# Opening stage: conditioning by feature tile on four column tiles of TensorE, with four projection units run tile by tile

## The chip, the cores and the metric

The kernel runs on one core of one Trainium2 chip. The metric is the device time of one execution in microseconds (us), the median of several runs. The core has five engines that run their own instruction streams and wait for each other by semaphores: TensorE (PE in the profile, its weight loads PEld), VectorE (DVE), ScalarE (ACT), GpSimd (POOL) and SyncE (SP, which issues nearly all transfers here).

## The reference, cut to what matters

Two transformer-like layers over 256 tokens of 1024 features. The change touches the start of the first:

```python
c_act = jax.nn.silu(c)                        # c: (1, 1024)
mod = c_act @ ada_w + ada_b                   # ada_w: (1024, 6144)
sh1, sc1, gt1, sh2, sc2, gt2 = jnp.split(mod, 6, axis=-1)
h = rmsnorm(x, mix_pre_g) * (1.0 + sc1) + sh1 # x: (256, 1024)
proj = h @ w_in                               # w_in: (1024, 10272)
```

Of `mod`, `h` needs the first two of six parts, 2048 columns of `ada_w` (8 MiB in fp32). Everything else in the layer needs `h`.

## The kernel before, in words

Activations lie feature-major: a tile is 128 features on the partitions by 256 tokens. The 1024 features of `x` and `h` are eight such tiles. The output features of each projection are cut into blocks of 128; one **unit** is such a block, computed from one chunk of weights of 128 x 1024 fp32 (512 KiB). Chunks pass through a ring of four slots: SP loads one (`load`), ACT rounds it to the matmul format (`high`, L1042, into `WH`), POOL subtracts to get the rest (`low`, L503, into `WL`), and PE multiplies. `h` is split the same way into `HH` and `HL`. A `triple` is the three matmuls `WH*HH`, `WH*HL`, `WL*HH` of one feature tile; a unit is eight triples, 24 matmuls, into one of four PSUM banks `psL`. SP loads a slot again once its chunk is split; ACT splits into a slot again once the unit that used it is done and its bank is read.

The opening, before: SP puts all transfers into one queue in the order of L407 to L430. ACT takes the silu of `c`, broadcast to all partitions, into `psO` (L1082). DVE takes each of 16 tiles of transposed `ada_w` (128 output features by 1024) as it lands, multiplies it with that row and sums (L1634); the sixteen sums are `mod[:, 0:16]`. From the tenth product's count on, PE runs 20 matmuls on constants whose result nobody reads (`fill`, L681). PE also sums the squares of `x` (`stat`, L678), ACT makes the reciprocal root of it (L1086, L1087). Once all sixteen products are there, DVE adds the bias, makes the gain `lead`, and `h` is made tile by tile by DVE, ACT and DVE (L1644, L1074, L1649). PE runs units 0 and 1 together, tile by tile as `h` is made (`together`, L603), then units 2 to 23 one after the other. Unit 24 follows behind a small projection `dt` (24 matmuls into `psS`). The first stage of the layer's projection, with its convolution on ACT (L1099) and DVE (L1676), runs beside these units, and with it DVE multiplies further tiles of `ada_w` with the row in `psO` (L1628).

## Time and profile before

| | |
|---|---|
| median of 3 runs | 1103.64 us (1101.42, 1103.64, 1114.60) |
| the profiled execution | 1113.12 us |
| its span, first to last instruction | 1111.3 us |
| mean granted clock of TensorE in it | 0.986 of full speed |
| PE busy | 1051.7 us, 95% of the span |
| DVE, ACT, POOL busy | 51%, 58%, 62% |
| DMA: bytes, mean rate over the span | 226.84 MB, 204 GB/s |

The profiled execution lies 9.5 us above the median of the runs and within their spread. All durations below are from it. Busy time of PE counts overlapping matmuls as busy once; it says when PE had work, not how well it used it.

### The profile page before, as it was taken

The numbers are of one execution on the slowest core, as the hardware profiler recorded it, in microseconds if no ns is written. First come the engines' busy times: TensorE is split into PE (matmuls) and PEld (weight loads), VectorE is DVE, ScalarE is ACT, GpSimd is POOL, SyncE is SP. The second block draws the span as 40 slices with busy tenths as digits, with TensorE's granted clock in tenths as the row PEclk, the third lists the DMA queues.
The fourth block names the chain that finished last, engine by engine and source line by source line (L and its number), as shares of the span: only waits on it lengthen the run. The fifth ranks groups of instructions, "written<-read, shape, count | busy, mean of one in ns | idle before, by whom it ended". The sixth has DMA issues, their size and how long they took to land.

```text
span 1111.3 us, 22886 instructions
## 1 busy us (share of the span) xinstructions
PE 1051.7 (95%) x8357; PEld 993.7 (89%) x8357; DVE 562.8 (51%) x1165; ACT 642.6 (58%) x1140; POOL 692.6 (62%) x306
## 2 busy tenths in 40 slices
PE   3999999999899989999999999998998889999998
PEld 2999999988789979999998999896665689999998
DVE  5877425589774454555423432495263724444400
ACT  3555754477764576666546557735576546666532
POOL 0787888812268847888786487660220065888795
PEclk9999999999999999999999999999899999999999
DMA  9988677656427855676677387567211033555463
GB/s 372 380 283 287 245 292 285 224 184 209 168 99 268 263 204 171 228 242 223 217 258 252 110 286 278 174 206 293 98 40 38 1 117 129 195 186 188 162 208 106
DMA packets 63650, 226.84 MB, mean 204 GB/s; under 512 B 6976, under 2 KB 8160, under 8 KB 63328
## 3 DMA queue, kind: packets, MB, share of 16 engines
q1 hardware_dynamic: 62384, 221.74, 57.1%
q10 hardware_dynamic: 1200, 4.23, 1.3%
q8 instruction: 40, 0.66, 0.2%
q14 instruction: 26, 0.21, 0.1%
HBM read 224.86 MB, written 1.08 MB: 203 GB/s over the span
## 4 chain that ended last, share of the span: by engine, by line
PE 67%; issue 16%; POOL 8%; ACT 3%; DMA 2%; DVE 2%; SPq 1%; POOLq 0%; ACTq 0%; DVEq 0%
PE psL L550 64%; POOL WL L503 8%; DMA R<-ada_w 1%; PE psS L550 1%; PE psO L550 1%; DMA ring<-wts 1%; SPq L405 1%; ACT WH L1042 1%; ACT R L1153 0%; ACT L1033 0%; ACT HR L1074 0%; SPq L390 0%; POOL R L530 0%; PE psS L839 0%; DVE HR L1649 0%
## 5 line engine op out<-in xcount | busy, mean ns | idle before, releaser
L503 POOL TENSOR_TENSOR WL<-ring,WH 128x1024 fp32r<-128x1024 f32 (+1 forms) x282 | 672.2, 2398 | 306.4 <-ACT WH L1042 245.5
L550 PE MATMUL psL<-HR,WH 128*128 128x256 f32 x3056 | 545.4, 281 | 5.7 <-POOL WL L503 2.5
L550 PEld LDWEIGHTS psL<-HR,WH 128*128 128x128 f32 x3056 | 468.2, 188 | 10.3 <-POOL WL L503 4.4
L550 PE MATMUL psL<-HR,WL 128*128 128x256 f32 x1528 | 428.1, 280 | 0.0
L550 PEld LDWEIGHTS psL<-HR,WL 128*128 128x128 f32 x1528 | 288.3, 189 | 0.0
L1042 ACT ACTIVATE WH<-ring 128x1024 fp32r<-128x1024 f32 (+1 forms) x210 | 216.1, 1040 | 100.9 <-PE psL L550 84.5
L550 PE MATMUL psL<-RR,WH 128*128 128x256 f32 x1344 | 240.8, 282 | 6.1 <-POOL WL L503 4.5
L550 PEld LDWEIGHTS psL<-RR,WH 128*128 128x128 f32 x1344 | 206.9, 189 | 7.7 <-issue 3.9
L550 PE MATMUL psL<-RR,WL 128*128 128x256 f32 x672 | 188.8, 281 | 0.0
L1328 ACT ACTIVATE WH<-ring 128x1024 fp32r<-128x1024 f32 (+1 forms) x88 | 92.9, 1055 | 86.8 <-PE psL L550 86.8
L1909 DVE SCALAR_TENSOR_TENSOR CT<-psL,par,CT 128x254 f32<-128x254 f32 (+1 forms) x176 | 81.0, 480 | 116.7 <-ACT CT L1331 111.3
L1628 DVE SCALAR_TENSOR_TENSOR adaring<-adaring,psO 128x1024 f32<-128x1024 f32 x80 | 96.8, 1217 | 70.9 <-DMA adaring<-ada_w 66.8
L550 PEld LDWEIGHTS psL<-RR,WL 128*128 128x128 f32 x672 | 127.1, 189 | 0.0
L550 PE MATMUL psL<-WH,HR 128*128 128x256 f32 (+1 forms) x320 | 55.0, 279 | 0.7 <-DVE HR L1649 0.7
L530 POOL TENSOR_TENSOR R<-R 128x256 f32<-128x256 f32 x16 | 14.5, 907 | 57.8 <-DVE R L1758 57.8
L550 PEld LDWEIGHTS psL<-WH,HR 128*128 128x128 f32 x320 | 48.6, 188 | 1.0 <-issue 0.9
L1331 ACT ACTIVATE CT<-psL,par 128x256 f32<-128x256 f32 x88 | 48.2, 548 | 0.0
L550 PE MATMUL psS<-SQ,par 128*128 128x256 f32 x90 | 27.9, 471 | 20.5 <-ACT SQ L1084 14.9
L550 PE MATMUL psL<-WL,HR 128*128 128x256 f32 (+1 forms) x160 | 44.5, 278 | 0.0
L550 PEld LDWEIGHTS psS<-SQ,par 128*128 128x128 f32 x90 | 20.7, 239 | 25.9 <-issue 17.5
L2222 DVE SCALAR_TENSOR_TENSOR X<-psL,mod,X 128x256 f32<-128x256 f32 x16 | 7.7, 484 | 67.9 <-PE psL L550 67.6
L1676 DVE SCALAR_TENSOR_TENSOR R<-psL,par,R 128x255 f32 (+2 forms) x72 | 34.7, 481 | 14.3 <-DVE R L1676 13.5
(255 smaller groups left out, 1103.5 us busy)
## 6 DMA issues: line engine op xcount, KB each, us to landing
ring<-wts SPq DMA_DIRECT2D x289, 512.0 KB, 3.7
adaring<-ada_w SPq DMA_DIRECT2D x80, 512.0 KB, 4.8
R<-ada_w SPq DMA_DIRECT2D x16, 512.0 KB, 12.6
ring<-wts SPq DMA_DIRECT2D x16, 384.0 KB, 3.4
R<-cum_dram ACTq DMA_DIRECT2D x8, 512.0 KB, 4.3
ring<-wts SPq DMA_DIRECT2D x8, 288.0 KB, 3.7
adaring<-wts SPq DMA_DIRECT2D x1, 2048.0 KB, 9.4
WHF<-wts SPq DMA_DIRECT2D x2, 1024.0 KB, 7.8
```

The source lines that it names most:

```text
L405: sp.dma_start(ADA0[n], ada_w[n * P:(n + 1) * P, :]).then_inc(ada_first[n], 16)
L503: nc.gpsimd.tensor_tensor(WL[:, k, 0:n], ring[:, k, 0:n], WH[:, k, 0:n].bitcast(F32), SUB).then_inc(lo_done, 1)
L530: G.tensor_tensor(Z[:, j, :], XBC[:, j, :], Z[:, j, :], MUL).then_inc(y_ready, 1)
L550: return nc.tensor.matmul(out, lhsT, rhs, start=start, stop=stop)
L1042: A(WH[:, k, 0:n], ring[:, k, 0:n], ACT.Copy).then_inc(hi_done, 1)
L1328: A(WH[:, q % SLOTS, 0:n], ring[:, q % SLOTS, 0:n], ACT.Copy).then_inc(hi_done, 1)
L1331: A(CT[:, 2 * slot + b, :], psL[:, u % 4, 0:T], ACT.Identity, scale=par[:, bass.ds(w0 + 2 * 44 + b * KF + j + it, 1)], bias=par[:, bass.ds ...
L1628: V.scalar_tensor_tensor(w, w, 1.0, cond, MUL, MUL, accum_out=col).then_inc(ada_used, 1)
L1676: ins = V.scalar_tensor_tensor(dst, psL[:, (u0 + k) % 4, 0:T - back], par[:, bass.ds(m + (c_w + (3 - back) * NXBC), 1)], dst, MUL, ADD)
L1909: ins = V.scalar_tensor_tensor(dst, psL[:, us[b] % 4, 0:T - back], par[:, bass.ds(w0 + (2 - back) * 44 + b * KF + j + it, 1)], dst, MUL, ADD)
L2222: V.scalar_tensor_tensor(X[:, m, :], lin(u), gates[:, m:m + 1], X[:, m, :], MUL, ADD).then_inc(lin_free[u % 4], 1)
```

## The change

The sixteen tiles of `ada_w` become eight of 1 MiB. Each holds, for one feature tile of `h`, its 128 columns of shift and 128 of gain, with the 1024 inputs in eight groups on the partitions. `CPAD` holds the silu of `c` as eight columns, each padded with zeros to 32. `ada_row(j)` multiplies them on PE: 32 x 256 outputs, the eight groups on four column tiles of the array in turn, so that four partial sums lie at partitions 0, 32, 64 and 96 of a bank of `psS`. ACT copies them to SBUF (`ROW`); `ada_col(j)` turns and sums them with two matmuls against a column of ones; DVE adds the bias and makes the gain of that tile, and tile `j` of `h` is made at once. `first_units(k)` runs the triples of feature tile `k` for units 0 to 3 together. The row of silu values that stays in `psO` for the later products is now made from eight diagonal blocks (DVE) and two matmuls with ones (`cond_rows`), no longer by a transfer of `c` to all partitions. Chunks 1 and 3 are subtracted by DVE (`first_low`) instead of POOL. The `fill` matmuls go. The transfers are reordered, and the parameters come in three parts instead of two.

```diff
--- before.py
+++ after.py
@@ -146,10 +146,11 @@
 
 PAR_SPEC = [
 
-    ("c_2", 8), ("ada_b", 48), ("mix_pre_g", 8), ("ones", P),
-
-    ("ident", P), ("w_dt", KD * HEADS1), ("mix_post_g", 8),
-    ("xconv_w", 4 * NXBC), ("xconv_b", NXBC), ("dskip", 16), ("ssd_norm_g", 16), ("sconv_w", 24),
+    ("c_1", 8), ("c_2", 8), ("ada_b", 48), ("mix_pre_g", 8), ("ones", P), ("ident", P),
+
+    ("xconv_w", 4 * NXBC), ("xconv_b", NXBC), ("w_dt", KD * HEADS1),
+
+    ("mix_post_g", 8), ("dskip", 16), ("ssd_norm_g", 16), ("sconv_w", 24),
...
-PAR_FIRST = PAR["ident"][0]
-
-
-def build(nc, x_t, par_in, c_row, ada_w, wts, out_t):
+PAR_FIRST, PAR_MID = PAR["xconv_w"][0], PAR["mix_post_g"][0]
+
+
+def build(nc, x_t, par_in, ada_w, wts, out_t):
...
-        ADA0 = [R[:, n * ADA_COLS + (0 if n < 14 else 4096):(n + 1) * ADA_COLS + (0 if n < 14 else 4096)] for n in range(ADA_FIRST)]
-        CROW = R[:, 20480:21504]
+        ADA0 = [R[:, n * 2048 + (0 if n < 7 else 4096):(n + 1) * 2048 + (0 if n < 7 else 4096)] for n in range(KD)]
+        DIAG1 = CT[:, :, :].rearrange("p a b -> p (a b)")
+        CPAD = RS[:, 1, :].rearrange("p (k m) -> p k m", m=32)
+        ROW = region(SQ, 0, a=2, b=T)
...
                     else:
-                        sp.wait_ge(lo_done, PLAN.split_at[before] + 1 + i * per)
+                        sp.wait_ge(lo_done, max(PLAN.split_at[before] + 1, SLOTS) + i * per)
...
-
-            sp.dma_start(CROW, c_row.rearrange("a b -> (a b)").partition_broadcast(P)).then_inc(c_in, 16)
+                rows = ada_w[n * 2 * P:(n + 1) * 2 * P, :].rearrange("(p a) n -> p (a n)", a=2)
+                sp.dma_start(ADA0[n], rows).then_inc(ada_first[n], 16)
+
             sp.dma_start(par[:, 0:PAR_FIRST], par_in[:, 0:PAR_FIRST]).then_inc(par_in_sem, 16)
-            for n in range(4):
-                load_first(n)
             sp.dma_start(X[:, :, :], x_t).then_inc(x_in, 16)
-            for n in range(4, 10):
-                load_first(n)
             load(0)
-            for n in range(10, 13):
-                load_first(n)
+            load_first(0)
             load(1)
-            for n in range(13, 16):
-                load_first(n)
+            sp.dma_start(par[:, PAR_FIRST:PAR_MID], par_in[:, PAR_FIRST:PAR_MID]).then_inc(par_mid_in, 16)
+            load_first(1)
             load(2)
             load(3)
-            sp.dma_start(par[:, PAR_FIRST:NPAR], par_in[:, PAR_FIRST:NPAR]).then_inc(par2_in, 16)
+            for n in range(2, KD):
+                load_first(n)
             load(4)
             load(5)
+            sp.dma_start(par[:, PAR_MID:NPAR], par_in[:, PAR_MID:NPAR]).then_inc(par2_in, 16)
             load_ada(16)
...
-            lows(0, PAIR_Q)
+            low(0)
+            low(2)
+            lows(SLOTS, PAIR_Q)
...
-            def cond_rows(diag):
-
-                pe.wait_ge(diag_ready, 1)
+            def cond_rows(diag, use):
+
+                pe.wait_ge(diag_ready, use)
                 for half in range(2):
...
+            cond_rows(DIAG1, 1)
             pe.wait_ge(sq_ready, 1)
             stat("stat_mix", sq_at, 8)
-            for n in range(12, 17):
-                pe.wait_ge(ada_used, n)
-                fill(0, 4)
-            linear8("in1", 0, 24, h_hi, h_lo, from_count(h_ready, 0), 2)
+
+            def ada_row(j):
+
+                pe.wait_ge(cpad_ready, 1)
+                pe.wait_ge(ada_first[j], 16)
+                if j >= 1:
+                    pe.wait_ge(col_read, j)
+                for k in range(KD):
+                    r = 32 * (k % 4)
+                    last = mm(psS[r:r + 32, 1, 0:T], CPAD[:, k, :], ADA0[j][:, k * T:(k + 1) * T], k < 4, k >= 4)
+                last.then_inc(row_done, 1)
+
+            def ada_col(j):
+
+                pe.wait_ge(row_ready, j + 1)
+                for e in range(2):
+                    last = mm(psS[:, 1, T + e:T + e + 1], ROW[:, j % 2, e * P:(e + 1) * P], pv("ones", 0, 1), True, True)
+                last.then_inc(col_done, 1)
+
+            def first_units(k):
+
+                pe.wait_ge(h_ready, k + 1)
+                if k == 0:
+                    pe.wait_ge(lo_done, SLOTS)
+                for c in range(SLOTS):
+                    last = triple(psL[:, c, 0:T], WH[:, c, k * P:(k + 1) * P], WL[:, c, k * P:(k + 1) * P],
+                                  HH[:, k, :], HL[:, k, :], k == 0, k == 7)
+                    if k == 7:
+                        last.then_inc(lin_done, 1)
+
+            for j in range(KD):
+                ada_row(j)
+                if 2 <= j < 7:
+                    first_units(j - 2)
+                if j == 7:
+                    first_units(6)
+                ada_col(j)
+                if j == 6:
+                    first_units(5)
+            first_units(7)
+            linear8("in1", SLOTS, 24 - SLOTS, h_hi, h_lo)
...
-            act.wait_ge(consts_ready, 1)
+            act.wait_ge(consts_ready, 2)
+            A(CPAD[:, :, 0:1].rearrange("p k m -> p (k m)"), pv("c_1"), ACT.Silu).then_inc(cpad_ready, 1)
             A(csil[:, :], pv("c_2"), ACT.Silu).then_inc(csil_ready, 1)
-            act.wait_ge(c_in, 16)
-            A(psO[:, :, :].rearrange("p a b -> p (a b)"), CROW, ACT.Silu).then_inc(cbc_ready, 1)
             act.wait_ge(x_in, 16)
             A(SQ[:, :], wide(X[:, :, :]), ACT.Square).then_inc(sq_ready, 1)
+            high(0)
             act.wait_ge(s_done, SCRATCH["stat_mix"] + 1)
             st.link(A(RS[:, 0, :], sbank("stat_mix")[:, 0:T], ACT.Ln, scale=1.0 / D, bias=eps_col[:, :]))
             A(sbank("stat_mix")[:, 0:T], RS[:, 0, :], ACT.Exp, scale=-0.5).then_inc(rs_ready, 1)
-            for c in range(2):
-                high(c)
-            make_hh(mod[:, 0:8], 0, first_t)
+
+            for j in range(KD):
+                act.wait_ge(row_done, j + 1)
+                A(ROW[:, j % 2, :], psS[:, 1, 0:T], ACT.Copy).then_inc(row_ready, 1)
+                act.wait_ge(t_ready, j + 1)
+                A(HH[:, j, :], CT[:, j % 4, :], ACT.Identity, bias=mod[:, j:j + 1]).then_inc(hh_ready, 1)
+                if j == 0:
+                    high(1)
+                if j == 1:
+                    high(2)
+                    high(3)
+                if j == 3:
+                    act.wait_ge(par_mid_in, 16)
+                    A(WDT[:, 0, :], pv("w_dt"), ACT.Copy).then_inc(wdt_hi, 1)
             fed[0] = SLOTS
-            act.wait_ge(par2_in, 16)
-            A(WDT[:, 0, :], pv("w_dt"), ACT.Copy).then_inc(wdt_hi, 1)
...
+            def diagonals(diag, silu):
+
                 for k in range(KD):
-                    st.mark(V.tensor_scalar(diag[:, k * P:(k + 1) * P], pv("ident"), csil[:, k:k + 1], None, MUL))
+                    st.mark(V.tensor_scalar(diag[:, k * P:(k + 1) * P], pv("ident"), silu(k), None, MUL))
...
-            dve.wait_ge(cbc_ready, 1)
-            for n in range(ADA_FIRST):
-                first = n + 8 if n < 8 else n - 8
-                dve.wait_ge(ada_first[n], 16)
-                V.scalar_tensor_tensor(ADA0[n], ADA0[n], 1.0, cond, MUL, MUL, accum_out=mod[:, first:first + 1]
-                                       ).then_inc(ada_used, 1)
-
-            def make_h(shift, gains, rs, base, t_at=None):
-
-                slots = 2 if t_at else 4
+            def make_h(shift, gains, rs, base):
+
                 for j in range(KD + 1):
                     if j < KD:
-                        if j >= slots:
-                            dve.wait_ge(h_ready, base + j - slots + 1)
-                        V.scalar_tensor_tensor(t_at(j) if t_at else CT[:, j % 4, :], X[:, j, :], gains[:, j:j + 1], rs, MUL,
+                        if j >= 4:
+                            dve.wait_ge(h_ready, base + j - 3)
+                        V.scalar_tensor_tensor(CT[:, j % 4, :], X[:, j, :], gains[:, j:j + 1], rs, MUL,
                                                MUL).then_inc(t_ready, 1)
                     if j >= 1:
                         n = j - 1
                         dve.wait_ge(hh_ready, base + n + 1)
-                        V.scalar_tensor_tensor(HL[:, n, :], t_at(n) if t_at else CT[:, n % 4, :], shift[:, n:n + 1], HH[:, n, :].bitcast(F32),
+                        V.scalar_tensor_tensor(HL[:, n, :], CT[:, n % 4, :], shift[:, n:n + 1], HH[:, n, :].bitcast(F32),
                                                ADD, SUB).then_inc(h_ready, 1)
 
-            dve.wait_ge(ada_used, ADA_FIRST)
             dve.wait_ge(par_in_sem, 16)
-            V.tensor_tensor(mod[:, 0:16], mod[:, 0:16], pv("ada_b", 0, 16), ADD).then_inc(mod_ready, 1)
-            dve.wait_ge(mod_ready, 1)
-            st.link(V.scalar_tensor_tensor(lead[:, 0:8], mod[:, 8:16], 1.0, pv("mix_pre_g"), ADD, MUL))
-            dve.wait_ge(x_in, 16)
-            dve.wait_ge(rs_ready, 1)
-            make_h(mod[:, 0:8], lead[:, 0:8], sbank("stat_mix")[:, 0:T], 0, first_t)
+            dve.wait_ge(cpad_ready, 1)
+            diagonals(DIAG1, lambda k: CPAD[:, k, 0:1])
+
+            def first_low(c):
+
+                dve.wait_ge(hi_done, c + 1)
+                V.tensor_tensor(WL[:, c, :], ring[:, c, :], WH[:, c, :].bitcast(F32), SUB).then_inc(lo_done, 1)
+
+            rows2 = lambda view, j: view.rearrange("p (a b) -> p a b", b=KD)[:, :, j:j + 1].rearrange("p a b -> p (a b)")
+            for j in range(KD):
+                dve.wait_ge(col_done, j + 1)
+                V.tensor_tensor(rows2(mod[:, 0:16], j), psS[:, 1, T:T + 2], rows2(pv("ada_b", 0, 16), j), ADD).then_inc(col_read, 1)
+                dve.wait_ge(col_read, j + 1)
+                st.link(V.scalar_tensor_tensor(lead[:, j:j + 1], mod[:, 8 + j:9 + j], 1.0, pv("mix_pre_g", j, 1), ADD, MUL))
+                if j == 0:
+                    dve.wait_ge(cbc_ready, 1)
+                    dve.wait_ge(x_in, 16)
+                    dve.wait_ge(rs_ready, 1)
+                V.scalar_tensor_tensor(CT[:, j % 4, :], X[:, j, :], lead[:, j:j + 1], sbank("stat_mix")[:, 0:T], MUL,
+                                       MUL).then_inc(t_ready, 1)
+                dve.wait_ge(hh_ready, j + 1)
+                V.scalar_tensor_tensor(HL[:, j, :], CT[:, j % 4, :], mod[:, j:j + 1], HH[:, j, :].bitcast(F32),
+                                       ADD, SUB).then_inc(h_ready, 1)
+                if j < 2:
+                    first_low(2 * j + 1)
+                if j == 4:
+                    dve.wait_ge(par_mid_in, 16)
+                    dve.wait_ge(wdt_hi, 1)
+                    V.tensor_tensor(WDT[:, 1, :], pv("w_dt"), WDT[:, 0, :].bitcast(F32), SUB).then_inc(wdt_ready, 1)
             dve.wait_ge(t_ready, 8)
             dve.sem_inc(s_free[SCRATCH["stat_mix"] % 2], 1)
-            dve.wait_ge(par2_in, 16)
-            dve.wait_ge(wdt_hi, 1)
-            V.tensor_tensor(WDT[:, 1, :], pv("w_dt"), WDT[:, 0, :].bitcast(F32), SUB).then_inc(wdt_ready, 1)
-            V.tensor_copy(identb[:, :], pv("ident")).then_inc(consts_ready, 1)
-            V.tensor_copy(maskb[:, :], pv("causal_add")).then_inc(consts_ready, 1)
+            dve.sem_inc(mod_ready, 1)
+            dve.sem_inc(ada_used, ADA_FIRST)
...
-    return np.concatenate([a[D:2 * D], a[0:D], a[2 * D:], b])
+    w = i["ada_w"][0][:, 0:2 * D].reshape(KD, P, 2, KD, P)
+    return np.concatenate([w.transpose(3, 1, 0, 2, 4).reshape(2 * D, D), a[2 * D:], b])
```

Not shown: new semaphores and their counts, `diagonals` called for the second layer as before, two small casts and the wait for the last part of the parameters moved behind the first loop of convolutions.

PE's first rows, before (`psS<-SQ,par` is `stat`, `psL<-par` is `fill`, `psL<-HR,WH` and `psL<-HR,WL` are the triples of `together`):

```order
L547 UNCONDITIONAL_BRANCH
L550 MATMUL psS<-SQ,par 128x256 x8
L550 MATMUL psL<-par 128x128 x20
L550 MATMUL psL<-HR,WH 128x256 x2
L550 MATMUL psL<-HR,WL 128x256
```

And with the change (`psO<-CT,par` is `cond_rows`, `psS<-R,RS` is `ada_row`, `psS<-par,SQ` is `ada_col`):

```order
L550 MATMUL psO<-CT,par 128x512 x2
L550 MATMUL psS<-SQ,par 128x256 x8
L550 MATMUL psS<-R,RS 32x256 x8
L550 MATMUL psS<-par,SQ 128x1 x2
L550 MATMUL psS<-R,RS 32x256 x8
L550 MATMUL psS<-par,SQ 128x1 x2
L550 MATMUL psS<-R,RS 32x256 x8
L550 MATMUL psL<-HR,WH 128x256 x2
L550 MATMUL psL<-HR,WL 128x256
```

`ada_row` of tiles 0, 1 and 2 stands ahead of the first triple; `ada_col` of tile 2 stands behind the four triples of feature tile 0.

ACT's rows from the silu on, before (`SQ<-X` the squares, `RS` and `psS<-RS` the root, `WH<-ring` is `high`, `HR<-psL,mod` makes `HH`):

```order
L1080 ACTIVATE csil<-par 128x8
L1082 ACTIVATE psO<-R 128x1024
L1084 ACTIVATE SQ<-X 128x2048
L1086 ACT_TABLE_LOAD
L1086 ACTIVATE RS<-psS,eps_col 128x256
L1087 ACT_TABLE_LOAD
L1087 ACTIVATE psS<-RS 128x256
L1042 ACTIVATE WH<-ring 128x1024 x2
L1074 ACTIVATE HR<-psL,mod 128x256 x3
```

And with the change, from the squares on (`SQ<-psS` is the copy into `ROW`):

```order
L1119 ACTIVATE SQ<-X 128x2048
L1080 ACTIVATE WH<-ring 128x1024
L1122 ACT_TABLE_LOAD
L1122 ACTIVATE RS<-psS,eps_col 128x256
L1123 ACT_TABLE_LOAD
L1123 ACTIVATE psS<-RS 128x256
L1127 ACTIVATE SQ<-psS 128x256
L1129 ACTIVATE HR<-CT,mod 128x256
L1080 ACTIVATE WH<-ring 128x1024
L1127 ACTIVATE SQ<-psS 128x256
L1129 ACTIVATE HR<-CT,mod 128x256
L1080 ACTIVATE WH<-ring 128x1024 x2
```

Chunk 0 is rounded ahead of the root, chunk 1 behind tile 0 of `h`, chunks 2 and 3 behind tile 1; the copy of a tile's sums stands behind the previous tile's `HH`.

## Rows read from the trace of the kernel before

**Rows 1.** Busy time by stage; columns: busy us of each engine, PEclk, DMA share, GB/s.
```profile
20.00:40.00 20.00, 14.90 (x83) 12.82 (x83) 16.52 (x34) 9.85 (x16) 8.19 (x4) 0.83 1.02 414
```

**Rows 2.** Chain of waits in the opening: start us, us, what; matmuls counted.
```profile
15.44 15.33 DMA R<-ada_w
...
39.77 63.87 PE psL L550 x540
103.63 2.77 PE psS L550 x24
```

**Rows 3.** SP's first issues of ada_w (start, us), and issues with us to landing.
```profile
1.66 1.90 SPq L405 DMA_DIRECT2D R<-ada_w  x4
...
R<-ada_w SPq DMA_DIRECT2D x1, 512.0 KB, 4.8
...
par<-params SPq DMA_DIRECT2D x1, 96.0 KB, 4.0
```

**Rows 4.** Timeline of ACT and PE (start us, us); last, durations of four `stat` records.
```profile
12.87 1.91 ACT L1084 ACTIVATE SQ<-X 128x2048 f32<-128x2048 f32 x1 [6.49 <-DMA X<-x_t]
...
14.92 6.64 PE L550 MATMUL psS<-SQ,par 128*128 128x256 f32 x16 [14.92 <-ACT SQ L1084]
...
21.60 0.47 ACT L1086 ACTIVATE RS<-psS,eps_col 128x256 f32<-128x256 f32 x1 [5.52 <-PE psS L550]
...
23.39 0.39 ACT L1087 ACTIVATE psS<-RS 128x256 f32<-128x256 f32 x1
...
L550 PE MATMUL psS<-SQ,par x4: 379/458/635, 20.2 to 21.2; 128*128 128x256 f32 x4
```

**Rows 5.** Groups by line and shape: busy us, mean ns of one, idle before.
```profile
L1617 DVE TENSOR_SCALAR HX<-par,csil 128x128 f32<-128x128 f32 x8 | 1.6, 271 | 0.0
...
L1654 DVE TENSOR_TENSOR mod<-mod,par 128x16 f32<-128x16 f32 x1 | 0.2, 175 | 0.0
...
L1644 DVE SCALAR_TENSOR_TENSOR psL<-X,lead,psS 128x256 f32<-128x256 f32 x8 | 3.8, 489 | 0.2
...
L1649 DVE SCALAR_TENSOR_TENSOR HR<-psL,mod,HR 128x256 fp32r<-128x256 f32 x8 | 3.8, 481 | 0.2
...
L1074 ACT ACTIVATE HR<-psL,mod 128x256 fp32r<-128x256 f32 x8 | 3.7, 471 | 6.3 <-DVE psL L1644 6.3
...
L1343 ACT ACTIVATE RR<-psS 128x256 f32 x32 | 11.9, 372 | 0.0
...
L1099 ACT ACTIVATE R<-psL,par 128x256 f32 x24 | 13.5, 563 | 29.0 <-PE psL L550 29.0
...
L1042 ACT ACTIVATE WH<-ring 128x1024 fp32r<-128x1024 f32 x195 | 203.8, 1055 | 79.6 <-PE psL L550 63.3 <-issue 9.3 <-DMA ring<-wts 2.9
```

**Rows 6.** Subtractions of 128 x 1024 on DVE (ns min/median/max), and one on POOL.
```profile
L1764 DVE TENSOR_TENSOR WL<-ring,WH x16: 1212/1224/1226, 234.0 to 290.2; 128x1024 fp32r<-128x1024 f32 x16
...
L1816 DVE TENSOR_TENSOR RR<-R,RR x4: 1211/2836/3194, 307.9 to 328.3; 128x1024 fp32r<-128x1024 f32 x4
...
38.91 2.39 POOL L503 TENSOR_TENSOR WL<-ring,WH 128x1024 fp32r<-128x1024 f32 x1 [0.47 <-ACT WH L1042]
```

**Rows 7.** Fp32 matmuls with 32 columns of weights (ns min/median/max), then a timeline.
```profile
L550 PE MATMUL psL<-adaring,HX x32: 378/379/404, 779.9 to 781.4; 128*32 128x256 f32 x32
L550 PE MATMUL psL<-WHF,HX x32: 378/379/380, 781.6 to 783.2; 128*32 128x256 f32 x32
...
786.08 0.63 PE L550 MATMUL psS<-par,SQ 128*128 128x30 f32 x4 [0.82 <-ACTq L1483]
786.64 0.64 PE L550 MATMUL psL<-ring,HX 128*32 128x256 f32 x8
```

**Rows 8.** Short stretches around changes of the granted clock; columns as in rows 1.
```profile
24.20:24.40 0.20, 0.00 (x0) 0.00 (x0) 0.15 (x3) 0.20 (x1) 0.00 (x0) 0.79 0.92 369
31.00:31.20 0.20, 0.20 (x3) 0.20 (x3) 0.20 (x1) 0.00 (x0) 0.00 (x0) 0.65 1.02 410
...
796.00:804.00 8.00, 8.00 (x37) 7.57 (x37) 3.04 (x9) 2.12 (x9) 0.00 (x0) 0.50 0.00 1
```

34 lines of the change are left out of this document (17 added, 17 removed).

## The prediction

> **What bounds the kernel now.** I read three views in this order. The busy times by stage show where PE is not full: over the span it is busy 95%, and between 20 and 40 us only 14.9 of 20 us [rows 1], with the transfers at their limit. The chain of waits shows why: up to 30.8 us it hangs on the last tile of `ada_w`, and from 39.77 us it is one unbroken run of 540 matmuls on PE, then `dt` [rows 2]. That run gives the unit's price, 24 x 63.87 / 540 = 2.84 us, and an anchor: `dt` begins at 103.6 us, 20 units behind the start of unit 4, so **unit 4 starts at 103.6 - 20 x 2.84 = 46.9 us**. From there PE is the chain, and the change leaves the units from 4 on as they are. So its whole effect is the shift of unit 4's start.
>
> **Transfers.** The first tile of `ada_w` lands at 1.66 + 4.8 = 6.5 us, the sixteenth at 30.8 [rows 2, 3]; between them 9.5 MiB go through the queue (7.5 of `ada_w`, 1 of `x`, two chunks), 2.56 us per MiB. `x` lands at 12.9 [rows 4]. The change puts 11.34 MiB up to its last tile instead of 10.59 (`c` broadcast away, two chunks and 0.25 of parameters more), so tile 7 lands at 30.8 + 0.75 x 2.56 = 32.7 us. Backwards by the same rate: tile 6 at 30.1, tile 2 at 19.9, tile 1 at 14.8, tile 0 at 10.5, chunks 2 and 3 by 17.3, `x` at 6.6. The first parameters, which took 4.0 us behind another transfer [rows 3], I put at 4.1.
>
> **Removed.** The sixteen products on DVE wait for transfers and hide behind them; without them nothing starts earlier, since their place is taken by the steps below. The `fill` matmuls fill idle time; what they cover is the clock, below. Each is priced at nothing by itself.
>
> **Up to the first tile of h.** Silu and hops 0.3, eight diagonals 1.6 [rows 5]: `cond_rows` starts at about 6.1. It streams half the columns that `stat` streams, and `stat` took 6.64 us at the lower clock level (1.2 GHz: its records last 635 ns, against 379 at the end, at 2.4) [rows 4], so 3.3 us, to 9.4. Squares are ready at 6.6 + 1.9 = 8.5, so `stat` waits for `cond_rows`. In the run before, the short records come some 6 us after PE began. From 6.1 that is 12, so `stat` takes 2.6 us slow and 2.0 fast: 14.0. From its end to the root are 23.39 + 0.39 - 21.6 = 2.2 us [rows 4]: 16.2. `ada_row(0)` is done under it; the copy (0.37) [rows 5] brings 16.6, `ada_col` (nearest row: four narrow fp32 records in 0.63 [rows 7]) 17.3. Then bias, gain, `t`, `HH`, `HL` at 0.17, 0.17, 0.49, 0.47, 0.48 [rows 5] with 0.2 of hops, 2.0 us: tile 0 of `h` at 19.3.
>
> **The new wait.** Triples may start only when four low parts are done. ACT does chunk 1 behind `HH(0)`: 18.8 to 19.9 [rows 5]. Then its copy for tile 1, `ada_col(1)` to 20.9; DVE is meanwhile in `first_low(1)`, 1.22 us [rows 6], to 21.1; `HH(1)` ends at 22.5, chunks 2 and 3 are rounded by 23.6 and 24.7. POOL's low part of chunk 2 takes 2.4 us, to 26.0 [rows 6]. DVE's of chunk 3 overlaps it. A DVE subtraction of that size with both inputs in SBUF takes 1.22 us while POOL does nothing, and 2.8 in the middle where POOL subtracts too [rows 6]; so I let it start when POOL ends: **first triples at 27.2 us**. Queued behind that wait on PE stand `ada_col(2)` and all later tiles, although tile 6 has nearly landed. PE had `ada_row(2)` at 21.3 and then nothing for almost 5 us. Before, the clock fell at 24.3, 2.7 us after `stat` [rows 4, 8]; so it is at the lower level here.
>
> **The loop from then on.** Per tile, PE does `ada_row`, 12 matmuls, `ada_col`, and waits for DVE's bias step before the next `ada_row`. Column tiling is in the trace: 32 records with 32 columns of weights start every 1.7 us [rows 7], so 16 take 0.87 us, a quarter of full width. Twelve matmuls are 1.42 us; with 0.63 and 0.2 for `ada_col` and the bias, the period is **3.1 us at full clock, above the 2.56 of a transfer**: this loop is bound by PE's own round trip, and ACT (0.9 us per tile) and DVE (2.0) fit in it. At the lower level the 12 matmuls take 2.84; of `ada_row` no row shows its price there, between 0.87 (if the weight loads set it) and 1.75; I take 1.75, since full-width matmuls at that level take twice as long, and that is the nearer operation than a weight load. So: triples 0 to 30.0, bias of tile 2 at 30.9, `ada_row(3)` to 32.6. There the clock rises, some 5.5 to 6 us after the work began, as before [rows 4, 8]. Triples 1 and the column give 34.8; tiles 4 and 5 at 3.1 each, 41.0. Then `ada_row(6)` 41.9, triples 4 43.3, triples 5 behind the column 45.1, `ada_row(7)` and triples 6 47.4, column 48.0, tile 7 of `h` 50.0, unit 0 done 50.5.
>
> **Behind the loop.** All four banks and slots come free together. Unit 4 needs bank 0 read (0.56), chunk 4 rounded (1.05) and subtracted (2.4), 4.1 with hops [rows 5, 6], three of them with PE idle: **unit 4 at 54.6 us**. Before, this handover was hidden, because units 0 and 1 ended before 2 and 3. Chunk 4 lands at 34.0 and waits; the following chunks, at 2.4 per low part against 2.84 per unit, keep up.
>
> **Sum.** 54.6 - 46.9 = **+7.7 us**. Against the profiled execution that is 1120.8; it lies 9.5 above the median, so the forecast is 1103.6 + 7.7 = **1111 us**.
>
> **A rule against the trace.** In the trace, 32-column matmuls start at 786.64 while full-width ones run until 786.71 [rows 7]: I see no pause at the switch, and charge none. The Trainium skill (TensorEngine Tiling (Array Packing), Key Properties) says that changing the tiling mode drains TensorE. By that rule each of the two switches per tile would cost the tail of a record, 0.38 less the 0.21 between two starts at full clock (half of 6.64 / 16 [rows 4, 7]), 0.17 us, and the five periods on the path would make the sum 9.4 instead of 7.7; this is an estimate with that page's rule and the 379 ns of the row.
>
> **Rivals.**
> - *The clock does not fall, or DVE and POOL do not collide.* Triples at 26.0 and full clock bring `ada_row(3)` to 28.2, three periods bring `ada_row(6)` to 37.5 instead of 41.0, then the same tail: unit 4 at 51.1, **+4.2, 1108**. With only one of the two it is +5.4 to +6.5. For it: PE has small pieces of work between 17 and 22. Against: 5 us without any.
> - *The transfers set the pace after all* (faster). If the low parts are done by 20 us and a period fits into 2.56, the triples ride on the landings: tile 7 at 32.7, row and triples 6 to 35.0, column 35.6, `h` 37.6, unit 0 done 38.1, handover 4.1: unit 4 at 42.2, **-4.7, 1099**. It needs the period below 2.56, a step cheaper than every row says, and the chain to the fourth low part 6 us shorter. It decides at the first triple: below 20 us with the short period it is a gain; with a period of 3.1 the start would have to be before 22.
> - *The clock stays at 1.2 GHz through the loop* (slower). Between 796 and 804 us the engine works without a pause and stays at 0.50 [rows 8], in small matmuls as `ada_col` and `ada_row` are. Period 1.75 + 2.84 + 0.8 = 5.4: `ada_row(3)` at 30.9, `ada_row(6)` at 47.1, tile 7 of `h` at 62.1, unit 0 done 63.0, unit 4 at 67.1: **+20.2, 1124**. If it lasts one more unit, 2.84 us more, it passes 2%. Against: the idle-time matmuls raised it at 31.1 [rows 8], and this loop keeps PE as busy as they did.
>
> **How the numbers follow.** Forecast 0.47, first rival (all its variants) 0.25, faster rival 0.13, slow clock 0.11 (a third of it in its long form), something else 0.04. The range runs from 1099 to 1120: it takes in the forecast with either price of the unknowns, the first rival, and the runs' own spread (1101 to 1115 for one kernel), and about half of the faster rival; it leaves the slow clock out. A difference counts as measured here beyond 2%, 22 us. No case reaches -22, and only the long form of the slow clock +22: faster 0.01, within 0.95, slower 0.04.
>
> **What would show it.** In the new profile: the first triple at 26 to 27.5 us and the fourth low part just before it; the idle of PE ahead of it; the granted clock at 0.5 there; `ada_row` starts 3.1 us apart, not 2.56; PE idle for about 3 us before unit 4; `dt` at 111, not 103.6. A first triple near 20 us, or periods of the landings' length, would refute the forecast.

## The result: 3% slower

The changed kernel takes **1137.23 us** (median of 4 runs, 1135.99 to 1138.22); the kernel before took 1109.12 beside it (4 runs, 1101.42 to 1114.74). The ratio is **1.0313**, 95% interval 1.0248 to 1.0378. Forecast were 1111 us and a range to 1120, with 0.04 for this side. The prediction was wrong.

The chain of waits of the changed kernel from the handover on; its second and third rows answer to the last two of [rows 2] (start us, us, what; matmuls counted). Behind it stands the row of the kernel before that answers to its fourth:

```profile
54.69 2.35 POOL WL L501
...
57.09 59.34 PE psL L550 x480
116.43 2.74 PE psS L550 x24
119.18 115.20 PE psL L550 x960
```

```profile
106.41 113.08 PE psL L550 x960
```

Unit 4 starts at 57.09 us; before it was 46.9, so the opening is 10.2 us longer up to there (forecast 7.7). `dt` begins at 116.43 instead of 103.63: 12.8 later. But the span is 24.3 us longer (1135.6 against 1111.3), so about half the loss is *behind* the opening, in code that the change leaves alone: the 960 matmuls behind `dt` alone take 115.20 us instead of 113.08. Four stretches of steady matmuls show it. The kernel before, and then the changed one (us from:to, length, busy time and records of PE, then of the weight loads, DVE, ACT, POOL; granted clock, DMA share, GB/s):

```profile
65.00:95.00 30.00, 30.00 (x258) 30.00 (x257) 21.87 (x44) 15.99 (x21) 25.49 (x12) 1.00 0.86 286
120.00:160.00 40.00, 40.00 (x342) 40.00 (x341) 13.85 (x21) 28.55 (x39) 34.65 (x15) 1.00 0.77 280
500.00:600.00 100.00, 100.00 (x851) 100.00 (x850) 38.56 (x80) 57.02 (x88) 83.91 (x38) 1.00 0.70 239
1010.00:1090.00 80.00, 80.00 (x681) 80.00 (x681) 22.51 (x52) 41.42 (x61) 67.38 (x31) 1.00 0.55 182
```

```profile
65.00:95.00 30.00, 30.00 (x252) 30.00 (x251) 21.90 (x46) 16.33 (x22) 25.45 (x11) 1.00 0.85 280
120.00:160.00 40.00, 40.00 (x336) 40.00 (x335) 19.76 (x33) 29.61 (x43) 30.29 (x14) 1.00 0.69 245
500.00:600.00 100.00, 100.00 (x835) 100.00 (x834) 44.27 (x94) 57.38 (x93) 81.88 (x37) 1.00 0.67 228
1010.00:1090.00 80.00, 80.00 (x669) 80.00 (x668) 30.70 (x72) 46.16 (x75) 66.06 (x29) 1.00 0.54 178
```

PE has no idle time and the clock is at 1.00 in all eight rows, and yet 1.8 to 2.3% fewer matmuls fit into each: three of them take 0.360 us from start to start instead of 0.353. No busy share says this; only the count beside it does.

The opening itself, on PE (start, us, operation, records; last, idle time before it and what ended it). The eight fp32 matmuls of an `ada_row` leave sixteen records:

```profile
8.79 4.50 PE L550 MATMUL psS<-SQ,par 128*128 128x256 f32 x16
13.22 1.07 PE L550 MATMUL psS<-R,RS 128*32 128x256 f32 x16
...
20.54 1.94 PE L550 MATMUL psS<-R,RS 128*32 128x256 f32 x16 [0.35 <-DVE mod L1703]
26.24 0.77 PE L550 MATMUL psL<-HR,WH 128*128 128x256 f32 x2 [3.76 <-DVE WL L1698]
28.94 0.85 PE L550 MATMUL psS<-par,SQ 128*128 128x1 f32 x4
30.13 1.94 PE L550 MATMUL psS<-R,RS 128*32 128x256 f32 x16 [0.34 <-DVE mod L1703]
...
35.46 1.07 PE L550 MATMUL psS<-R,RS 128*32 128x256 f32 x16 [0.35 <-DVE mod L1703]
36.46 0.50 PE L550 MATMUL psL<-HR,WH 128*128 128x256 f32 x2
...
38.00 0.50 PE L550 MATMUL psS<-par,SQ 128*128 128x1 f32 x4
38.85 1.07 PE L550 MATMUL psS<-R,RS 128*32 128x256 f32 x16 [0.35 <-DVE mod L1703]
...
51.81 0.79 PE L550 MATMUL psL<-HR,WH 128*128 128x256 f32 x2 [2.03 <-DVE HR L1713]
57.09 0.50 PE L550 MATMUL psL<-HR,WH 128*128 128x256 f32 x2 [2.35 <-POOL WL L501]
```

The first triples wait 3.76 us for a low part and start at 26.24. The rows of 32-column matmuls take 1.94 us at the lower clock and 1.07 at the full one; at full clock the next one starts 3.39 us later. DVE's low parts, whose second one runs beside POOL's from 22.67 to 25.01:

```profile
18.89 1.23 DVE L1698 TENSOR_TENSOR WL<-ring,WH 128x1024 fp32r<-128x1024 f32 x1 [0.46 <-ACT WH L1080]
...
23.57 2.52 DVE L1698 TENSOR_TENSOR WL<-ring,WH 128x1024 fp32r<-128x1024 f32 x1 [1.41 <-ACT WH L1080]
```

1.23 us alone, 2.52 beside POOL, of which 1.44 lie under POOL's: what is left after POOL's end is 1.08. The Trainium skill (SBUF — State Buffer, "SBUF: two separate sides") says that such a subtraction and a GpSimd operation take the ports that they share by turns and whole. These rows agree but for 0.15 us: by that rule a whole subtraction, 1.23, would be left, and 1.08 is. The granted clock (columns as above):

```profile
20.00:34.00 14.00, 9.54 (x58) 6.97 (x59) 5.21 (x10) 3.56 (x6) 2.34 (x1) 0.50 1.02 420
34.00:36.00 2.00, 1.65 (x21) 1.48 (x23) 0.78 (x3) 0.00 (x0) 0.00 (x0) 0.88 1.02 426
36.00:50.00 14.00, 13.09 (x136) 10.70 (x128) 4.87 (x16) 3.76 (x9) 0.00 (x0) 1.00 0.65 259
...
52.00:54.00 2.00, 2.00 (x10) 2.00 (x11) 0.04 (x1) 0.90 (x2) 0.00 (x0) 0.50 0.00 0
...
58.00:60.00 2.00, 2.00 (x13) 2.00 (x12) 1.64 (x4) 0.81 (x1) 2.00 (x2) 0.59 0.82 260
60.00:62.00 2.00, 2.00 (x12) 2.00 (x11) 1.20 (x4) 0.16 (x1) 2.00 (x2) 0.56 0.72 225
```

It is at the lower level (1.2 GHz) from about 18 to 34 us, and falls twice more: in the last triples, behind the 2 us that PE waited for `h`, and in unit 4, behind the waits of the handover.

### The profile page after: what moved, and what is told of

The parts are those of the page before. It is cut to its first block, busy times and chain, and to the rows that moved or that the text cites. A ratio compares the mean times of both kernels' runs of the same rounds, so it can differ in the third digit from the quotient of the medians.

```text
span 1135.6 us, 23102 instructions
## 1 busy us (share of the span) xinstructions
PE 1079.9 (95%) x8481; PEld 1015.2 (89%) x8481; DVE 550.5 (48%) x1158; ACT 644.3 (57%) x1148; POOL 685.4 (60%) x304
## 3 DMA queue, kind: packets, MB, share of 16 engines
HBM read 224.34 MB, written 1.08 MB: 199 GB/s over the span
## 4 chain that ended last, share of the span: by engine, by line
PE 66%; issue 20%; POOL 8%; ACT 3%; DVE 1%; DMA 1%; POOLq 0%; ACTq 0%; DVEq 0%; SPq 0%
PE psL L550 63%; POOL WL L501 8%; PE psS L550 1%; PE psO L550 1%; DMA ring<-wts 1%; ACT WH L1080 0%; DMA X<-x_t 0%; ACT R L1199 0%; ACT L1071 0%; POOL R L530 0%; PE psS L877 0%; DVE CT L1943 0%; DVE X L1944 0%; ACT RS L1069 0%; ACT RS L1071 0%
## 5 line engine op out<-in xcount | busy, mean ns | idle before, releaser
L501 POOL TENSOR_TENSOR WL<-ring,WH 128x1024 fp32r<-128x1024 f32 (+2 forms) x280 | 665.0, 2389 | 337.1 <-ACT WH L1080 270.1
L550 PE MATMUL psL<-HR,WH 128*128 128x256 f32 x3056 | 560.5, 284 | 12.4 <-POOL WL L501 4.6
L550 PEld LDWEIGHTS psL<-HR,WH 128*128 128x128 f32 x3056 | 477.9, 191 | 19.5 <-issue 8.7
L550 PE MATMUL psL<-HR,WL 128*128 128x256 f32 x1528 | 434.9, 285 | 0.0
L550 PE MATMUL psL<-RR,WH 128*128 128x256 f32 x1344 | 243.8, 283 | 5.4 <-POOL WL L501 4.1
L1929 DVE TENSOR_TENSOR CT<-CT,psS 128x256 f32<-128x256 f32 x21 | 8.8, 421 | 65.0 <-ACT psS L1331 59.5
L550 PE MATMUL psL<-ring,R 128*128 128x192 f32 (+1 forms) x128 | 31.5, 395 | 2.2 <-DMA ring<-wts 2.2
```

Source lines behind the costliest of these rows:

```text
L501: nc.gpsimd.tensor_tensor(WL[:, k, 0:n], ring[:, k, 0:n], WH[:, k, 0:n].bitcast(F32), SUB).then_inc(lo_done, 1)
L550: return nc.tensor.matmul(out, lhsT, rhs, start=start, stop=stop)
L1929: ins = V.tensor_tensor(SUMS, SUMS, psS[:, m % 2, 0:T], ADD).then_inc(sq_added, 1)
```

## The experiments

Sixteen kernels ran, in four groups; each group was timed beside its own runs of the kernel before, each group on another chip, and only ratios to those are compared. What could make an untouched stream of matmuls slower? The change also makes `par` 8 columns wider (c_1 is added), so every buffer behind it in SBUF (X, SQ, the buffer HR of HH and HL, R, CT, RS) moves by 32 bytes, while the weight buffers ring, WH, WL and `adaring` stay ahead of it. **Theory L**: this shift costs the stream. **Rival O**: the opening costs everything.

**First group: dead columns, and two units.**

`e1`, the kernel before (`e2` has 16 in place of 8):

```diff
-        par = sb("par", [P, NPAR])
+        par = sb("par", [P, NPAR + 8])
```

> The kernel before, with the parameter buffer 8 columns (32 bytes per partition) longer, nothing read there. In the changed kernel the parameters grew by 8 columns, and everything behind them in SBUF (x, h, the large work buffer) lies 32 bytes further on. Layout theory: this alone makes every matmul that streams from those buffers slower, as in the changed kernel (836 matmuls in 100 us instead of 851), so this kernel is slower than before by 12 to 16 us, 1.012 to 1.014. Rival, the change's own instructions cause the slower pace: no difference, 1.000.

Measured: **1.0219** (1.0149 to 1.0289). Eight columns that nothing reads cost the kernel before 2.2%, more than the 1.2 to 1.4% expected. Its stretches are those of the changed kernel:

```profile
65.00:95.00 30.00, 30.00 (x252) 30.00 (x251) 21.40 (x44) 16.01 (x22) 25.27 (x11) 1.00 0.81 277
...
500.00:600.00 100.00, 100.00 (x836) 100.00 (x835) 41.72 (x88) 55.99 (x88) 81.81 (x37) 1.00 0.68 230
```

> The kernel before with the parameter buffer 16 columns (64 bytes) longer: the control of the 32-byte shift. Layout theory, if it is the 64-byte phase that counts: 1.000, and 851 matmuls in 100 us as before. If any shift costs: slower as with 8 columns.

Measured: 1.0119 (1.0042 to 1.0195), with 252 and 845 records in these stretches. A place at a multiple of 64 bytes is not what it needs.

`e3`, the changed kernel with the same edit, so that it too lies 64 bytes off:

> The changed kernel with the parameter buffer 8 columns longer, which puts the buffers behind it back on the 64-byte phase they had before. Layout theory: 12 to 16 us faster than the changed kernel, so 9 to 12 us slower than before, 1.009 to 1.011, the opening's own loss (unit 4 starts at 57.1 instead of 46.9). Rival: as the changed kernel, 1.022 to 1.031.

Measured: 1.0202 (1.0136 to 1.0269). Divided by 1.0119, that of `e2` with the same shift, the change proper is 1.008.

`e4`, as `e3`, but only units 0 and 1 in the loop, and all low parts on POOL:

```diff
-                    pe.wait_ge(lo_done, SLOTS)
-                for c in range(SLOTS):
+                    pe.wait_ge(lo_done, 2)
+                for c in range(2):
...
             first_units(7)
+            for c in (2, 3):
+                unit(c, c, 1, h_hi, h_lo)
...
-            low(0)
-            low(2)
-            lows(SLOTS, PAIR_Q)
+            lows(0, PAIR_Q)
...
-                if j < 2:
-                    first_low(2 * j + 1)
```

> The changed kernel, buffers back on the old phase, but only units 0 and 1 run tile by tile in the loop; units 2 and 3 follow as in the kernel before, and all four low parts are POOL's. The first triple waits for two low parts instead of four (about 21 us instead of 26.2), a period of the loop has 6 matmuls less per tile (2.7 instead of 3.4 us), and the rounding of chunk 4 is hidden behind units 2 and 3. Theory that the loop's four units cost the opening its gain: unit 4 starts at 43 to 45 us, 2 to 4 us earlier than before, 0.996 to 0.998. Rival, the conditioning on PE itself (waits between PE, ACT and DVE, the low clock) is too slow: unit 4 at 47 or later, 1.000 or more.

Measured: 1.0176 (1.0095 to 1.0256). The first triples start at 21.70, as expected, but from tile 1 on an `ada_row` takes 1.94 us, the tiles come 4.5 to 5.3 us apart, and `dt` begins at 115.72: 0.7 us earlier than with the change, 1.4 earlier than in `e3`, and 12 later than before. So the rival's side holds. The clock stays at 0.50 from 20 to 34 and at 0.55 from 34 to 48, although PE is busy 92 to 94% of that time:

```profile
20.00:34.00 14.00, 12.85 (x78) 8.54 (x73) 6.17 (x11) 4.65 (x9) 5.20 (x3) 0.50 1.02 427
34.00:48.00 14.00, 13.16 (x85) 9.06 (x85) 4.31 (x14) 2.68 (x6) 0.00 (x0) 0.55 0.76 309
```

**Second group: where the address counts.**

`e5`, the changed kernel with `par` at 3785 columns again, so that all large buffers lie where they lay before; c_2 is loaded straight into `csil`, and its silu comes behind `dt`:

```diff
-    ("c_1", 8), ("c_2", 8), ("ada_b", 48), ("mix_pre_g", 8), ("ones", P), ("ident", P),
+    ("c_1", 8), ("ada_b", 48), ("mix_pre_g", 8), ("ones", P), ("ident", P),
...
-    ("cmask_add", 2 * NCMP), ("cmask01", 2 * NCMP), ("sel", 2 * NCMP),
+    ("cmask_add", 2 * NCMP), ("cmask01", 2 * NCMP), ("sel", 2 * NCMP), ("c_2", 8),
...
-        par = sb("par", [P, NPAR])
+        par = sb("par", [P, NPAR - 8])
...
+            sp.dma_start(csil[:, :], par_in[:, NPAR - 8:NPAR]).then_inc(par2_in, 16)
...
-            A(csil[:, :], pv("c_2"), ACT.Silu).then_inc(csil_ready, 1)
+            A(csil[:, :], csil[:, :], ACT.Silu).then_inc(csil_ready, 1)
```

> The changed kernel with every large SBUF buffer at the address it has in the kernel before: of the 16 columns that carry the two conditioning vectors, c_2's 8 are kept in the small buffer csil and loaded on their own, so that par is 3785 columns wide again. Theory L (the addresses cost the rest): the matmul stream goes back to 851 records in 500:600, the start of 'dt' stays about 116, and the median is 10 to 13 us above the kernel before (ratio 1.009 to 1.012). Rival O (the opening costs all of it and what follows is only a side of it): the median stays 25 to 28 us above (ratio 1.023 or more), at about 836 records in 500:600.

Measured: **1.0092** (1.0057 to 1.0128). Theory L's number; O falls. And 1.0092 x 1.0219 (`e1`) = 1.0313, the ratio of the change; that all the digits agree is luck, since the factors are uncertain by 0.4 and 0.7%. The chain from unit 4 on:

```profile
54.68 56.31 PE psL L551 x480
110.99 2.72 PE psS L551 x24
```

Unit 4 starts at 54.68, 2.4 us earlier than with the change. The first triples started 1.4 us earlier (24.82) and the last ones 2.0 (49.78), and the last ones ran at full clock; from the end of unit 0 on the handover takes 4.0 us in both. Two things came out against the forecast: `dt` at 111 instead of about 116, and a stream that is quicker than before, 267 records in 65:95 against 258 and 871 in 500:600 against 851. The profiled execution is also the quickest of this kernel's eleven (1107.28, median 1123.29); its pace is taken up with the table below.

`e6`, 8 dead columns ahead of all buffers; `e7`, 8 behind HR's buffer; `e8`, `par` 32 wider, all in the kernel before:

```diff
+        lead_pad = sb("lead_pad", [P, 8])
         ring = sb("ring", [P, SLOTS, SLOT])
```

> The kernel before with a dead buffer of 8 columns (32 bytes) ahead of all SBUF buffers, so that the weights WH and WL and the activations HH and HL move together and keep their distances. If the distance between the weights and the activations is what the matmul stream feels, the time is that of the kernel before (within 0.3%) and 851 records in 500:600. If it is the place of a buffer by itself (a multiple of 64 bytes, say), it is slower by 1 to 2%, as with 32 bytes behind par (1.022).

```diff
         HX = sb("HX", [P, 4096])
+        pad_r = sb("pad_r", [P, 8])
```

> The kernel before with 8 dead columns (32 bytes) behind the buffer of HH and HL: par, X, SQ, HH and HL stay, the buffer R of the activations (Z, XBC, G1, XTOK), CT and RS move by 32 bytes. If the addresses of HH and HL are what costs, no change in 500:600 if that stretch multiplies HH and HL. If it is the results in R, CT and RS, the whole loss of 1 to 2% is here.

```diff
-        par = sb("par", [P, NPAR])
+        par = sb("par", [P, NPAR + 32])
```

> The kernel before with par 32 columns (128 bytes) wider: everything behind par keeps its place within 128 bytes. If the pattern repeats by 128 bytes, the time is that of the kernel before; if not, it is 1 to 2% slower as with 32 (1.022) and 64 bytes (1.012).

Measured: `e6` 0.9963 (0.9926 to 0.9999), `e7` 1.0009 (0.9971 to 1.0047), `e8` **0.9837** (0.9793 to 0.9880). Moving everything together costs nothing, so it is not a buffer's place by itself but a distance. Moving R, CT and RS costs too little to see in the whole time, but the trace of `e7` shows it. Its first row below multiplies HH and HL, which did not move, its second a tile of R, which did; the rows behind are the kernel before in the same stretches (PE's busy time and records, granted clock, DMA share, GB/s):

```profile
960.00:1040.00 80.00, 80.00 (x682) 1.00 0.55 183
1050.00:1100.00 50.00, 50.00 (x419) 1.00 0.54 169
```

```profile
960.00:1040.00 80.00, 80.00 (x682) 1.00 0.55 183
1050.00:1100.00 50.00, 50.00 (x427) 1.00 0.55 179
```

In one execution, three matmuls take 0.353 us from the buffer that stayed and 0.360 from the one that moved by 32 bytes. R is read so for some 190 us in all, worth 3 to 4 us. And 128 bytes *gain* 1.6%, which I had not expected.

**Third group: HR alone, and the clock.**

`e9`, 8 dead columns between SQ and HR, in the kernel before:

```diff
+        pad_h = sb("pad_h", [P, 8])
         with nc.sbuf_tensor("HR", [P, 4096], F32R) as HR:
```

> The kernel before with 8 dead columns (32 bytes) between SQ and the buffer of HH and HL: par, X and SQ keep their addresses, HH, HL and all behind move by 32 bytes. Moving only R, CT and RS cost nothing (1.0009) and moving everything together cost nothing (0.9963), so what is left are par, X, SQ and HH/HL against the weight buffers. If the distance between WH/WL and HH/HL is it, the whole loss is here (ratio 1.015 to 1.025, about 252 matmul records in 65:95). If it is par, X or SQ, the time is that of the kernel before (within 0.5%, 257 or more records).

Measured: 1.0160 (1.0105 to 1.0215), 252 records. `par`, X and SQ have not moved; R, CT and RS have, and cost some 0.3% by `e7`. So at 32 bytes most of the loss belongs to the distance of **HH and HL** to the weight buffers. (The start of `par` has moved against HH and HL here and in `e1` as well, but these matmuls don't read it.) One triple after another of `e1`, and behind it of `e13` (below), at the same time; WH records come in twos:

```profile
520.05 0.40 PE L550 MATMUL psL<-HR,WH 128*128 128x256 f32 x2
...
520.41 0.40 PE L550 MATMUL psL<-HR,WH 128*128 128x256 f32 x2
```

```profile
520.11 0.39 PE L551 MATMUL psL<-HR,WH 128*128 128x256 f32 x2
...
520.45 0.39 PE L551 MATMUL psL<-HR,WH 128*128 128x256 f32 x2
```

A triple costs 0.36 us in the one and 0.34 in the other, from start to start.

`e10` is `e5` with short matmuls of ones in PE's waits, `e11` the same with two units in the loop (`e4` at the addresses of before), `e12` is `e11` with `par` 32 columns wider. The edit is shown for `e10`; in `e11` the counts are 7, 2, 3, 3, 3, 3, 3, 2 and 3, 4, 1, 1, 1, 1, 1, 0, without the 8:

```diff
+            def warm(count, free=True):
+                for _ in range(count):
+                    mm(psL[:, 3, 384:512], pv("ones"), pv("ones"), free, free)
...
+                if j == 2:
+                    warm(8)
                 if 2 <= j < 7:
                     first_units(j - 2)
...
+                warm([7, 2, 1, 1, 1, 1, 1, 1][j], ...)
                 ada_col(j)
+                warm([3, 6, 1, 1, 1, 1, 1, 0][j], ...)
...
+            warm(7, ...)
             first_units(7)
```

> The changed kernel at the addresses of the kernel before, with short matmuls of ones in TensorE's waits (7 and 3 around the first tile's row, 2, 6 and 8 until the first triples, 1 and 1 in each later tile, 7 ahead of the last triples); the results are not read. Theory C (half clock is why the opening took longer): the granted clock stays at 1.00 from 16 to 34, ada_row takes 1.07 us each time, the first triples still wait for the weights' low part until 24.5 to 26, unit 4 starts at 49 to 52 instead of 54.7, and the median is 3 to 5 us below that of the changed kernel at the same addresses (ratio to before 1.005). Rival W (the work in order on TensorE and its handshakes set it, not the clock): unit 4 at 54 or later, no gain.

Measured: 1.0069 (1.0022 to 1.0117), no difference from `e5`; unit 4 at 57.21, which is what rival W had said. The clock still fell, behind PE's wait of 1.84 us for the low part:

```profile
24.00:28.00 4.00, 2.18 (x16) 2.21 (x16) 1.68 (x1) 0.00 (x0) 0.60 (x1) 0.89 1.01 418
28.00:32.00 4.00, 4.00 (x27) 2.50 (x26) 1.28 (x4) 0.89 (x2) 0.00 (x0) 0.50 1.00 413
```

The tiles came 3.6 us apart (rows at 34.95, 38.54, 42.13) instead of 3.4, with the fill in PE's order. Theory C was not tested by it, because the clock wasn't held.

> As the run before it, but only units 0 and 1 are multiplied in the loop over the tiles (0.64 us a tile instead of 1.28) and units 2 and 3 run whole after it, with all low parts on POOL; 3 short matmuls fill each wait for a row. Theory C: at full clock a tile costs TensorE about 1.07 + 0.8 + 0.64 + 0.35 = 2.9 us, which is what the transfers take (2.93), so that the loop ends with them: unit 2 starts at 37 to 40 and unit 4 at 42 to 45, earlier than the 46.87 before; 'dt' starts near 99 to 101 and the ratio to the kernel before is 0.995 to 0.998. Rival W: unit 2 at 49 or later as with two units and no fill, ratio 1.01.

Measured: 1.0025 (0.9985 to 1.0065). Here the clock is held:

```profile
20.00:34.00 14.00, 12.73 (x132) 9.76 (x131) 7.13 (x16) 5.43 (x11) 5.43 (x3) 1.00 1.02 418
...
43.79 63.16 PE psL L549 x534
106.94 2.76 PE psS L549 x24
```

Full clock from 20 to 34 us, and the chain (last two rows) has `dt` at 106.94, 8.8 us earlier than `e4`, some 0.9 of it from the address (534 matmuls in 63.16 us; at three in 0.360 they take 64.1). So the low clock was worth most of the 12 us that separate the opening of `e4` from that of before, but the rest of my expectation failed: tiles came every 3.34 us, not 2.93, the last triples began at 43.79, and `dt` was still 3.3 us later than in the kernel before.

> The same kernel with par 32 columns (128 bytes) wider, the move that made the kernel before faster (0.9837). If the address term and the opening add up: 0.979 to 0.983. If the address term belongs to something in the kernel before alone: as the run before it.

Measured: **0.9852** (0.9790 to 0.9914), a little above the forecast. The gain of 128 bytes adds to the opening; the opening itself brings nothing over `e8`'s 0.9837.

**Fourth group: how far the address goes, and the last try of the opening.**

`e13` has 32 in place of 8 in the edit of `e9`; `e14` is the kernel before with `par` 64 wider; `e15` the changed kernel with `par` 24 wider (128 bytes in all).

> The kernel before with 32 dead columns (128 bytes) between SQ and the buffer of HH and HL: par, X and SQ stay. If the gain of par + 128 bytes (0.9837) is the distance of HH/HL to the weight buffers alone, the ratio is 0.980 to 0.988 here too, with about 708 matmul records in 1010:1090 instead of 681. If par, X or SQ have a part in it, the ratio is 0.995 to 1.000.

> The kernel before with par 64 columns (256 bytes) wider. With 32, 64 and 128 bytes the ratios were 1.022, 1.012 and 0.984. If distances repeat by 256 bytes, the ratio is 1.000 (0.996 to 1.004); if by 128 bytes from some point on, 0.984; else anything from 0.98 to 1.02, and the pattern is not a short one.

> The changed kernel as it is, with par 24 columns wider, so that everything behind par is 128 bytes from its place in the kernel before. If address and opening add up: 0.9837 x 1.0092 = 0.993 (0.989 to 0.997), faster than the kernel before although the same change measured 1.031. If they don't: 1.00 or more.

Measured: `e13` **0.9857** (0.9801 to 0.9913), `e14` 0.9990 (0.9941 to 1.0040), `e15` **0.9965** (0.9926 to 1.0004). `par`, X and SQ have no part in the gain either. At 256 bytes the whole time is as it was. The changed kernel, 3% slower as it stands, equals the kernel before when its buffers lie 96 bytes further on. In `e13` the forecast of 708 records in 1010:1090 can't be read (the quicker kernel ends before 1090). 1010:1080 shows the gain; first the kernel before, then `e13`:

```profile
1010.00:1080.00 70.00, 70.00 (x596) 70.00 (x596) 22.03 (x51) 37.40 (x57) 58.93 (x27) 1.00 0.55 181
```

```profile
1010.00:1080.00 70.00, 70.00 (x620) 70.00 (x619) 14.46 (x33) 33.28 (x45) 61.06 (x28) 1.00 0.56 182
```

`e16` is `e12` with PE and ACT reordered (the triples of tile 5 now stand behind the row of tile 7) and less fill:

```diff
-                warm([7, 2, 3, 3, 3, 3, 3, 2][j])
+                warm([7, 2, 2, 2, 2, 2, 2, 1][j])
...
-                if j == 1:
-                    high(2)
-                    high(3)
+                if j in (3, 4):
+                    high(j - 1)
...
-                if j == 6:
-                    first_units(5)
```

> Two units in the loop, all low parts on POOL, the high parts of units 2 and 3 behind tiles 3 and 4 instead of both behind tile 1, the triples of tile 5 behind the row of tile 7, two short matmuls a tile instead of four, the 128 bytes. Theory: col of tile 2 at about 21.7 instead of 24.0, a tile every 3.0 us instead of 3.3, unit 2 at 38 to 40 instead of about 44, 'dt' at 100 to 102.5 instead of 107.1 (the kernel before with the same 128 bytes: 104.7), ratio 0.979 to 0.983, 2 to 4 us below the kernel before with 128 bytes. Rival: the transfers or the handshakes hold the tile at 3.3 us, unit 2 at 42 or later, no gain over it.

Measured: 0.9883 (0.9832 to 0.9933), `dt` at 103.39. The rival holds: the last triples start at 42.59 and unit 2 behind them, and there is no gain over `e8`. (`dt` is 1.3 us earlier than the 104.70 of `e8`, but by the pace of the stream in this profile: 534 matmuls take 60.80 us here and 63.16 in `e12`, and with these `dt` would be at 105.8.) The handshakes set the tile. Rows on PE, without what lies between:

```profile
20.55 1.07 PE L549 MATMUL psS<-R,RS 128*32 128x256 f32 x16
...
23.65 1.07 PE L549 MATMUL psS<-R,RS 128*32 128x256 f32 x16 [0.34 <-DVE mod L1710]
...
26.74 1.07 PE L549 MATMUL psS<-R,RS 128*32 128x256 f32 x16 [0.34 <-DVE mod L1710]
...
30.37 1.07 PE L549 MATMUL psS<-R,RS 128*32 128x256 f32 x16 [0.34 <-DVE mod L1710]
33.57 0.61 PE L549 MATMUL psS<-par,SQ 128*128 128x1 f32 x4 [0.79 <-ACT SQ L1134]
34.52 1.07 PE L549 MATMUL psS<-R,RS 128*32 128x256 f32 x16 [0.34 <-DVE mod L1710]
```

The tiles are 3.1 us apart while ACT is free, and 3.6 and 4.2 where it has a chunk to round (1.04 us) ahead of the copy that `ada_col` waits for (the 0.79). No order tried here makes the opening by tiles better than that of the kernel before at the same addresses.

## The shift in one table

Ratios to the kernel before, by how far HH and HL moved against the weight buffers:

| shift | kernel before with it | changed kernel | quotient |
|---|---|---|---|
| 0 | 1 (`e6` 0.9963, all together) | 1.0092 (`e5`) | 1.009 |
| 32 bytes | 1.0219 (`e1`), 1.0160 (`e9`) | 1.0313 (the change) | 1.009 |
| 64 | 1.0119 (`e2`) | 1.0202 (`e3`) | 1.008 |
| 128 | 0.9837 (`e8`), 0.9857 (`e13`) | 0.9965 (`e15`) | 1.013 |
| 256 | 0.9990 (`e14`) | not run | |

The quotient, what the change costs apart from the shift, is 0.8 to 1.3% in each row, 9 to 14 us (1.5% with `e9` in place of `e1`); by the intervals of its two ratios each is uncertain by some 0.5 to 1%. The shift costs 18 to 24 us at 32 bytes (1.6 to 2.2% of 1109) and gives 16 to 18 back at 128.

The traces show what the whole times hide: how long three matmuls of the stream take from start to start, in ns, in four stretches at full clock.

| shift | kernel | 70 to 95 us | 125 to 210 | 450 to 580 | 1010 to 1080 |
|---|---|---|---|---|---|
| 0 | before | 353 | 353 | 353 | 353 |
| 0 | `e6`, `e11` | 353 | 340 | 353 | 353 |
| 0 | `e10` | 353 | 340 | 340 | 353 |
| 0 | `e5` | 340 | 340 | 340 | 353 |
| 256 | `e14` | 353 | 353 | 340 | 353 |
| R alone by 32 | `e7` | 353 | 353 | 353, from R 360 | 353, from R 360 |
| 32 | the change, `e1`, `e9` | 360 | 360 | 360 | 360 |
| 64 | `e2` | 360 | 356 | 356 | 360 |
| 64 | `e3`, `e4` | 360 | 356 | 356 | 356 |
| 128 | `e8` | 353 | 340 | 353 | 340 |
| 128 | `e12`, `e13` | 353 | 340 | 340 | 340 |
| 128 | `e15`, `e16` | 340 | 340 | 340 | 340 |

A stretch keeps its pace to its end, and the paces are few: 340, 353, 356 and 360 ns. The distance decides which of them occur. At 32 and 64 bytes all are slow; the last stretch is at 353 in each kernel at 0 or 256 bytes and at 340 in each at 128. But within one distance the other stretches are at 340 in some kernels and at 353 in others, and no run explains which. Nor is it known whether that changes from one execution to the next, since each kernel has one profile. It would fit `e5`: at 353 in the stretches of its first three columns its profiled execution would take some 13 us more, 1120, near its median, and it would fit the spread of one kernel's runs (1098 to 1121). Neither is shown.

Not settled either is *why* the distance counts: the runs show one that seems to repeat by 256 bytes, in four of eight possible 32-byte steps, and nothing on the circuit behind it. The traces narrow it down. In the last stretch of the kernel before (935 to 1107 us), three matmuls take 353 ns where ACT, POOL and DVE all work for over 90% of them (60 groups of three) and where all three are idle for over 90% (44 groups). In `e1` it is 360 in both cases (48 and 47 groups), in `e13` 340 (84 and 46). So what another engine does at that moment makes no difference. PE's own two reads, of weights and of activations, are the likeliest reading that is left, but no run shows them collide, and none takes away the transfers, which run all the time. The Trainium skill (SBUF — State Buffer, "SBUF: two separate sides") says that PE never waits on anyone for its ports; as far as the other engines go, these counts agree.

## Why the prediction was wrong

1. **"The change leaves the units from 4 on as they are. So its whole effect is the shift of unit 4's start."** This step failed. It read the instructions and not their addresses. Its missing term is the larger one: 1.0219 of 1.0313 (`e1`, `e5`). The diff showed it (`par` grows by 8 columns), and nothing in the profile of before prices it, since a profile has one layout only. The runs showed in its place a stream of matmuls that takes 360 ns per three where it took 353. My range had no term for "something global", so it ended at 1120. The opening alone, at unchanged addresses, gave 1.0092 x 1103.6 = 1114 us, within the range; forecast was 1.007.
2. **Up to the first triples: right, 0.9 to 1.0 us early.** First tile of `h` at 18.4 (forecast 19.3), first triples at 26.24 (27.2), behind DVE's low part that POOL held up. `stat` was short by its clock as assumed (4.50 us for 4.6). The new wait, with PE idle before it and the clock at 0.50, is as described. That makes the first rival wrong in both its conditions: the clock fell, and DVE and POOL did collide.
3. **"The period is 3.1 us at full clock": mis-sized.** It is 3.39 (35.46 to 38.85). From start to start, `ada_row` takes 1.00 (forecast 0.87), the triples 1.54 (1.42), column and bias 0.85 (0.83). At the lower level `ada_row` takes 1.87 to the next start (30.13 to 32.00), a little over the upper bound of 1.75. The two full periods alone make 0.6 us. The prediction's own step from 43.3 to 45.1 is 0.2 us short of its terms (0.63 + 1.42), and in the slow rival the same terms are 0.3 us short.
4. **"There the clock rises" at 32.6: late.** It rose at about 34.3, so the triples of tile 1 took 2.6 us (32.00 to 34.62) and not 1.42. This is the largest single miss inside the opening.
5. **The handover.** Its parts came as priced (evacuation 0.56, rounding 1.05, low part 2.35). Unit 0 ended at 53.1 (forecast 50.5). Of these 2.6 us the loop had brought 1.8 (last triples at 51.81, forecast 50.0); the rest is the last triples, made slow by a clock that had fallen in PE's wait. It fell again in unit 4. That unit 4 of `e5` starts at 54.68, as in the forecast of 54.6, is luck: there the first triples were 2.4 us ahead of the forecast, and the loop from there to the last triples was 2.2 too long. From unit 4 to `dt` the changed kernel takes 59.3 us and not 56.8: 1.05 by the address (`e1`: 65.05 for 540 matmuls instead of 63.87, for 480 of them), and 1.4 by the clock, since five triples of unit 4 between 58.60 and 61.79 take 0.64 us each instead of 0.36.
6. **The rule on mode switches** of the Trainium skill (TensorEngine Tiling (Array Packing), Key Properties) would have made it 9.4 instead of 7.7, and 10.2 was measured. That is no proof of it, since no run separated the switch, but charging nothing was too little. Records without a switch between them overlap by 0.17 us (0.38 long, 0.21 apart); those at 786.64 in [rows 7] overlap by 0.07, so 0.1 us was lost there, and the prediction read that as no pause. In the changed kernel four `ada_row` records start every 0.216 us, and the next matmul (36.46) starts 0.36 behind the last four: 0.14 more. Both are near the 0.17 of that estimate, and such pauses are part of the 3.39 us of point 3.
7. **The rivals.** "The clock stays at 1.2 GHz through the loop" did not come (it was at 1.00 from 36), and the transfers did not set the pace in any kernel, even with the clock held: 3.1 us was the shortest period (`e16`).

## What to carry to other kernels

When a change adds or widens a buffer, look at where every buffer behind it ends up, and run the *old* kernel with the same dead bytes before you judge the change: here that alone was 2%, over twice what the change itself cost, and the same knob, turned to 128 bytes, gave the fastest kernels of this study (0.984 to 0.986, no instruction touched). Count records in a stretch without idle time at full clock; it tells a slower stream from a longer path, which busy shares don't. Count them in several stretches, and compare medians of many runs too, because one stretch of one profile can be at either of two paces at the same distance. And a loop that hands each tile from PE to ACT to PE to DVE has a period of its own (3.1 to 3.4 us here), which transfers that were all in at 31.9 us (forecast 32.7) could not speed up.

## What the hardware showed that I had not expected

- Matmuls that stream without a gap at full clock take 340, 353, 356 or 360 ns per three, and a shift of the activations' buffer against the weights' decides which of these occur (`e9`, `e13`); the ends are 3.0% of the run apart (1.0160 to 0.9857). In `e7` two of these paces stand side by side in one execution, by the buffer that is read.
- PE can be busy 92% of 14 us and be granted only 0.50 (`e4`, 20 to 34 us); with short matmuls of ones in its waits it was at 1.00 in the same stretch, at a busy share of 91% (`e11`).
- Eight fp32 matmuls of 32 columns on four column tiles (sixteen records) take 1.07 us at full clock and 1.94 at half: the small tiles did not hide the clock.
